# Per-head mean squares as rows of tokens, inverse roots spread by one fp32r product, and two maps folded in the transposition

## The reference

```python
x += 1/2 * post(SwiGLU_1(pre(x)))
x += post(W_out [GLA | DiffAttn+ALiBi | Retention](pre(x)))
x += 1/2 * post(SwiGLU_2(pre(x)))
...
o_a = _rms_norm(o_a, P['gla_norm'][l]) * silu(gr)           # 4 heads of 64
s = jnp.where(visible, s - slopes * dist, NEG_INF)
p = jax.nn.softmax(s, axis=-1)
a = p[:, 0] - lam * p[:, 1]                                 # two maps
return jnp.einsum('bhqk,bkhv->bqhv', a, vf)
...
o_d = _rms_norm(o_d, P['diff_subln'][l]) * (1.0 - lam_init) # 4 heads of 128
o_r = _layer_norm(o_r, P['ret_norm'][l]) * silu(rg)         # 4 heads of 64
```

## Time and profile before

| | |
|---|---|
| median of three runs | 1440.01 us |
| the profiled execution: its time, its span | 1441.2 us, 1439.4 us |
| mean granted TensorE clock | 0.977 |
| busy: TensorE, VectorE, ScalarE, GpSimd | 95%, 56%, 43%, 9% |
| chain that ended last, by engine | TensorE 86%, VectorE 6%, DMA 3%, ScalarE 2% |
| multiplications L582 to L584, all | 8016, 2512.3 us busy as records, which overlap |

### The profile page before, as it was taken

How to read it: one execution, slowest core, us unless ns; L and a number is a source line. 1 busy time by engine, 2 the same in 40 slices (tenths; PEclk the granted TensorE clock), 3 DMA queues, 4 the chain that set the end, 5 groups by cost and what they waited for, 6 DMA issues and landing times.

```text
span 1439.4 us, 24605 instructions
## 1 busy us (share of the span) xinstructions
PE 1369.2 (95%) x9589; PEld 1331.6 (93%) x9589; DVE 812.5 (56%) x1226; ACT 625.0 (43%) x987; POOL 122.7 (9%) x119
## 2 busy tenths in 40 slices
PE   5999999899999899999989999998899999999998
PEld 5999999887799899999989999988788999999998
DVE  5565544568654765554366555346765557655542
ACT  4444433552353654443354444346234455444343
POOL 0000000341000200000020000013500002000000
PEclk9999999999999999999999999999999999999999
DMA  5955445433241365545545555454232343555452
GB/s 145 272 147 153 143 146 150 123 99 88 80 125 46 97 182 151 153 140 148 153 115 147 147 146 149 149 172 104 61 89 78 110 118 102 146 149 154 140 147 75
DMA packets 351289, 188.50 MB, mean 131 GB/s; under 512 B 6188, under 2 KB 348472, under 8 KB 350968
## 3 DMA queue, kind: packets, MB, share of 16 engines
q1 hardware_dynamic: 348368, 177.49, 43.9%
q0 software_dynamic: 1872, 6.88, 1.4%
q10 hardware_dynamic: 984, 3.22, 0.7%
HBM read 183.25 MB, written 4.33 MB: 130 GB/s over the span
## 4 chain that ended last, share of the span: by engine, by line
PE 86%; DVE 6%; DMA 3%; ACT 2%; DVEq 1%; issue 1%; POOL 0%; ACTq 0%; SPq 0%; POOLq 0%
PE ps L582 26%; PE ps L584 26%; PE ps L583 25%; DMA raw<-in_ffn_w_up_dram 2%; DVE scores L1399 2%; DVE w_l L938 1%; DMA raw<-in_w_in_dram 1%; PE ps L860 1%; PE ps L870 1%; PE ps L638 1%; PE ps L763 1%; PE ps L834 0%; PE ps L748 0%; DVE y L1254 0%; PE ps L881 0%
## 5 line engine op out<-in xcount | busy, mean ns | idle before, releaser
L582 PE MATMUL ps<-xn_l,w_h 128*128 128x320 f32 x1840 | 588.2, 320 | 25.4 <-DVE xn_l L1243 18.2
L583 PE MATMUL ps<-xn_h,w_l 128*128 128x320 f32 x1840 | 576.4, 313 | 0.0
L584 PE MATMUL ps<-xn_h,w_h 128*128 128x320 f32 x1840 | 576.3, 313 | 0.0
L938 DVE TENSOR_TENSOR w_l<-raw,w_h 128x1024 fp32r<-128x1024 f32 (+1 forms) x342 | 412.5, 1208 | 185.0 <-ACT w_h L929 184.9
L929 ACT ACTIVATE w_h<-raw 128x1024 fp32r<-128x1024 f32 (+1 forms) x342 | 353.4, 1035 | 278.3 <-DMA raw<-in_ffn_w_down_dram 125.2
L582 PEld LDWEIGHTS ps<-xn_l,w_h 128*128 128x128 f32 x1840 | 353.2, 192 | 35.7 <-DVE xn_l L1243 19.6
L583 PEld LDWEIGHTS ps<-xn_h,w_l 128*128 128x128 f32 x1840 | 353.5, 192 | 0.8 <-issue 0.2
L584 PEld LDWEIGHTS ps<-xn_h,w_h 128*128 128x128 f32 x1840 | 353.1, 192 | 0.0
L582 PE MATMUL ps<-hid_l,w_h 128*128 128x320 f32 x704 | 217.4, 309 | 0.0
L584 PE MATMUL ps<-hid_h,w_h 128*128 128x320 f32 x704 | 217.3, 309 | 0.0
L583 PE MATMUL ps<-hid_h,w_l 128*128 128x320 f32 x704 | 217.3, 309 | 0.0
(11 more groups left out here) (223 smaller groups left out, 1165.8 us busy)
## 6 DMA issues: line engine op xcount, KB each, us to landing
raw<-in_ffn_w_up_dram SPq DMA_DIRECT2D x176, 512.0 KB, 3.9
raw<-in_ffn_w_down_dram SPq DMA_DIRECT2D x64, 448.0 KB, 3.7
raw<-in_w_in_dram SPq DMA_DIRECT2D x54, 512.0 KB, 3.8
raw<-in_ffn_w_down_dram SPq DMA_DIRECT2D x32, 512.0 KB, 3.9
raw<-in_w_out_dram SPq DMA_DIRECT2D x16, 512.0 KB, 4.1
const<-in_tables_dram ACTq DMA_DIRECT2D x1, 2176.0 KB, 10.7
mask_in<-in_masks_dram POOLq DMA_DIRECT2D x1, 1536.0 KB, 11.7
x_in<-in_x_prompt_dram SPq DMA_DIRECT2D x1, 1024.0 KB, 3.6
```

The source lines that it names most:

```text
L582: pe.matmul(out, w_h[s][:, w], xl, start=first, stop=False)
L583: pe.matmul(out, w_l[s][:, w], xh, start=False, stop=False)
L584: return pe.matmul(out, w_h[s][:, w], xh, start=False, stop=last)
L938: dve.tensor_tensor(w_l[s][:, 0:cols], raw[s][:, 0:cols], w_h[s][:, 0:cols], ALU.subtract).then_inc(w_lo, 1)
```

## The change

1. `stat` takes constants as the stationary operand: for each tile of squares a matrix `mean` of 128x44 that holds 1/64 or 1/128 in the columns of its heads, twice, at c and at 32 + c. One multiplication of 320 columns per tile is accumulated, so that the means stand as rows of 320 tokens, on 44 partitions (rows that no head has are zero). Root and reciprocal are then of 44x320, and VectorE adds two steps: a cast of the inverse roots to fp32r, and, for rows 32 to 43, the inverse root less its cast. The tile `inv_2` so holds each head's inverse root in two fp32r parts. Each step is followed by a drain. Storage for these rows is taken from tiles that are no longer used.
2. `spread` is one fp32r multiplication: `pick`, a 44x128 matrix of ones at the head's two rows, by `inv_2` of 44x320.
3. For the sample `att_t` is a multiplication of `probs` by `fold` (128x64, two identities on top of each other) in place of the transposition: it transposes and adds the two maps. `att_o` then needs three multiplications where it had six, and ScalarE copies 3x64 columns where it copied 3x128.
4. The tables grow: the second transfer has 4768 columns where it had 4352 (128 partitions, fp32), and `pick` is loaded by GpSimd's queue, 44x1024, behind the masks. TensorE waits for it once before the mixer.

```diff
@@ -49,11 +49,9 @@
-HEAD_AT = ((0, 2, "head64"), (2, 2, "head64"), (8, 1, "head128"), (9, 1, "head128"), (10, 1, "head128"), (11, 1, "head128"),
-           (4, 2, "head64"), (6, 2, "head64"))
+HEAD_AT = ((0, 2), (2, 2), (8, 1), (9, 1), (10, 1), (11, 1), (4, 2), (6, 2))
 HEAD_ORDER = (2, 3, 4, 0, 1, 6, 7, 5)
 STAT_HEADS = {"a": (0, 1, 6, 7, 2, 3, 4), "b": (5,)}
-STAT_COLS = {"a": (0, 11), "b": (11, 12)}
 STAT_BANK = {"a": 3, "b": 6}
@@ -222,6 +219,17 @@
     add("bias", np.concatenate([bias(r, r), bias(128 + r, np.arange(256)), b2], axis=1))
+    mean, pick = np.zeros((P, 8, 44)), np.zeros((P, 8, P))
+    for q, (c, w) in enumerate(HEAD_AT):
+        for h in range(w):
+            rows = slice(h * P // w, (h + 1) * P // w)
+            for g in (0, 32):
+                mean[rows, q, g + c + h] = w / P
+                pick[g + c + h, q, rows] = 1.0
+    fold = (r[:, None] % 64 == np.arange(64)[None, :]).astype(np.float32)
+    add("mean", mean.reshape(P, -1))
+    add("fold", fold)
+    add("pick", pick.reshape(P, -1))
     masks = []
@@ -253,7 +261,9 @@
         N_PAR = 16 * 10
+        NCONST -= 8 * P
         const = sb("const", [P, NCONST])
+        pick = sb("pick", [P, 8, P], F32R)
         mask = sb("mask", [P, 8, 3 * P], U8)
@@ -332,8 +343,10 @@
         tiny = place("tiny", [P, 32])
-        var_h = place("var_h", [P, 3, 12])
-        inv_h = place("inv_h", [P, 3, 12])
+        root_h = {"a": z[0:64, DQ[2], :], "b": decay[0:64, :]}
+        inv_h = {"a": z[0:64, DKK[2], :], "b": wgt_0[0:64, :]}
+        inv_2 = {"a": nc.alloc_sbuf_tensor_at("inv_2a", [P, T], F32R, offset=z0 + 4 * DV[2] * T),
+                 "b": nc.alloc_sbuf_tensor_at("inv_2b", [P, T], F32R, offset=qk_at)}
         assert here[0] <= nc.sbuf_usable_end, (here[0], nc.sbuf_usable_end)
@@ -508,6 +522,7 @@
                     pool.dma_start(mask_in[:, :], ins["masks"]).then_inc(masks_loaded, 16)
+                    pool.dma_start(pick[0:44, :, :].rearrange("p a b -> p (a b)"), ins["tables"][0:44, NCONST:]).then_inc(pick_loaded, 16)
                     pool.wait_ge(masks_loaded, 16)
@@ -844,7 +859,11 @@
                     for kt in range(KEYS[ATT[n][1]]):
-                        mm = pe.transpose(ps[:, 6, kt * P:(kt + 1) * P], probs[:, n % 2, kt * P:(kt + 1) * P], C("ident"))
+                        p = probs[:, n % 2, kt * P:(kt + 1) * P]
+                        if ATT[n][1] < 2:
+                            mm = pe.transpose(ps[:, 6, kt * P:(kt + 1) * P], p, C("ident"))
+                        else:
+                            mm = pe.matmul(ps[:, 6, kt * P:kt * P + T_S], p, C("fold"), start=True, stop=True)
                     mark("pe", mm, f"att_t{n}")
@@ -854,32 +873,22 @@
                         v = vc[:, kt, h * P:(h + 1) * P] if b == 2 and kt < 2 else dv_tok[:, kt, h, :]
-                        for m in range(1 if b < 2 else 2):
-                            o, a = (ps[:, 7, b * P:(b + 1) * P], probs_t[:, kt, :]) if b < 2 else \
-                                   (ps[:, 7, 256:320], probs_t[:, kt, half_rows(m)])
-                            mm = pe.matmul(o, v, a, start=b == 0, stop=b < 2 and kt == b or kt == 2 and m == 1, skip_group_check=True)
+                        o, w = (slice(b * P, (b + 1) * P), P) if b < 2 else (slice(T_P, T), T_S)
+                        mm = pe.matmul(ps[:, 7, o], v, probs_t[:, kt, 0:w], start=b == 0, stop=kt == b, skip_group_check=True)
                     mark("pe", mm, f"att_o{n}")
...
                     for q in STAT_HEADS[n]:
-                        c, w, ind = HEAD_AT[q]
-                        for i in range(3):
-                            at = 12 * i + c
-                            mm = pe.matmul(ps[:, STAT_BANK[n], at:at + w], z[:, q, TOK[i]:TOK[i] + P], C(ind), start=True, stop=True,
-                                           skip_group_check=True)
+                        mm = pe.matmul(ps[0:44, STAT_BANK[n], 0:T], C("mean")[:, 44 * q:44 * q + 44], z[:, q, :],
+                                       start=q == STAT_HEADS[n][0], stop=q == STAT_HEADS[n][-1])
                     mark("pe", mm, f"ms_{n}")
...
                     j = HEAD_ORDER.index(n)
-                    c, w, _ = HEAD_AT[n]
                     after(pe, l, "dve", "inv_b" if n == 5 else "inv_a")
                     after(pe, l, "dve", f"head{HEAD_ORDER[j - 2]}" if j >= 2 else "att_max11")
-                    m = P // w
-                    for i in range(3):
-                        for h in range(w):
-                            mm = pe.matmul(ps[h * m:h * m + m, 4 + j % 2, TOK[i]:TOK[i] + P],
-                                           inv_h[:, i, c + h:c + h + 1].broadcast_to([P, m]), C("ident"), start=True, stop=True)
+                    mm = pe.matmul(ps[:, 4 + j % 2, 0:T], pick[0:44, n, :], inv_2["b" if n == 5 else "a"][0:44, :], start=True, stop=True)
                     mark("pe", mm, f"spread{n}")
@@ -1019,7 +1029,7 @@
                 if l == 0 and f == 0:
-                    act.dma_start(const[:, FIRST:], ins["tables"][:, FIRST:]).then_inc(tables_loaded, 16)
+                    act.dma_start(const[:, FIRST:], ins["tables"][:, FIRST:NCONST]).then_inc(tables_loaded, 16)
                 with act.Fori(1, KF // 3 - 1) as i:
@@ -1113,7 +1123,8 @@
                         after(act, l, "pe", f"att_o{n - 1}")
-                    mark("act", act.activation(probs_t[:, 0:keys, :], ps[:, 6, 0:keys * P].rearrange("p (k c) -> p k c", c=P),
+                    w = P if ATT[n][1] < 2 else T_S
+                    mark("act", act.activation(probs_t[:, 0:keys, 0:w], ps[:, 6, 0:keys * P].rearrange("p (k c) -> p k c", c=P)[:, :, 0:w],
                                                ACT.Copy), f"att_t{n}")
@@ -1130,10 +1141,8 @@
                 elif kind == "stat":
-                    a, b = STAT_COLS[n]
-                    src = ps[:, STAT_BANK[n], 0:36].rearrange("p (i c) -> p i c", i=3)
                     after(act, l, "pe", f"ms_{n}")
-                    mark("act", act.activation(var_h[:, :, a:b], src[:, :, a:b], ACT.Sqrt, bias=C("eps")), f"sqrt_{n}")
+                    mark("act", act.activation(root_h[n][0:44, :], ps[0:44, STAT_BANK[n], 0:T], ACT.Sqrt, bias=C("eps")[0:44, :]), f"sqrt_{n}")
                 elif kind == "gates":
@@ -1488,9 +1497,12 @@
                 elif kind == "stat":
-                    a, b = STAT_COLS[n]
                     after(dve, l, "act", f"sqrt_{n}")
-                    mark("dve", dve.reciprocal(inv_h[:, :, a:b], var_h[:, :, a:b]), f"inv_{n}")
+                    dve.reciprocal(inv_h[n][0:44, :], root_h[n][0:44, :])
+                    dve.drain()
+                    dve.tensor_copy(inv_2[n][0:44, :], inv_h[n][0:44, :])
+                    dve.drain()
+                    mark("dve", dve.tensor_tensor(inv_2[n][32:44, :], inv_h[n][32:44, :], inv_2[n][32:44, :], ALU.subtract), f"inv_{n}")
                 elif kind == "spread":
```

More of the change, by code:

```diff
@@ L189, in constants @@
     add("lam", np.tile(np.concatenate([lam, 1.0 - lam])[None, :], (P, 1)))
+    add("pad", np.zeros((P, 2)))
     add("mean64", np.kron(np.eye(2), np.ones((64, 64))) / 64.0)
-    add("head64", np.kron(np.eye(2), np.ones((64, 1))) / 64.0)
-    add("head128", np.ones((P, 1)) / 128.0)
     rot = np.zeros((P, P))
@@ L323, in build @@
         wgt_0 = place("wgt_0", [P, T])
+        qk_at = here[0]
         qk_0 = place("qk_0", [P, 2, T])
@@ L359, in build @@
         tables_loaded = sem("tables_loaded")
+        pick_loaded = sem("pick_loaded")
         masks_loaded = sem("masks_loaded")
@@ L893, in _ @@
                 pe.wait_ge(tables_loaded, 16)
+                pe.wait_ge(pick_loaded, 16)
                 for kind, *arg in SCHEDULE:
```

## The result

The changed kernel takes 1448.7 us (median of 16 runs, 1444.2 to 1453.9), the kernel before beside it 1440.2 (16 runs, 1438.0 to 1447.6): 1.0059 times as long, with a 95% interval of 1.0049 to 1.0070. That is 8.5 us more. The forecast was 0.8 us less, so it was wrong by 9.3 us and on the wrong side. The ratios further down leave out two of the 21 runs of the kernel before that stand beside the last experiments, 1567.8 and 1685.3 us, whose mean granted clock was 0.81 and 0.75. The profiled execution took 1447.3 us, its span is 1445.5 (before 1439.4), the mean granted clock 0.972 (before 0.977). TensorE's share of the chain fell from 86% to 84%, VectorE's rose from 6% to 8%.

What follows compares the result with a forecast made beforehand. TensorE was taken as the bound, with VectorE setting the pace in places. Statistics and spreads -5.3, maps -2.5, clock +5.0, constants +2.0 gave -0.8 us: 1439.2 us predicted, range 1431 to 1446.

Steps and rivals of the forecast that it cites:

- VectorE's chain: Behind each statistics: root 0.43 to 0.48 us, reciprocal 2.1, cast 0.35, difference 0.48, gaps 0.2.
- Rival 3: VectorE's chain is longer and the kernel slower: 1446.8 us at 12 ns per column; chance 0.10 in the slower form.
- The statistics: Statistics `a` at the mixer's end: 14 records of 0.27 us, 3.8 us in all, without lowering the clock.
- TensorE's wait ahead of the spreads: After statistics `a`, TensorE waits 1.7 us for the inverse roots.
- Constants: Larger tables lengthen TensorE's wait in the first FFN by 1.0 us, clock fall costs 1.0: 2.0 us lost.
- Maps: Folded sample maps in the attention heads save 0.41 us per head, 2.5 us for three heads in two layers.
- rival 1: The clock stays up at these places and in the first FFN: 1433.2 us; chance 0.18.
- rival 2: TensorE's saving counts in full, with reciprocals ready in time: 1426 us; chance 0.14.
- both places that were named: Clock falls expected around 434.2 to 440.5, before `out` 0, and in the gap of about 4 us before `out` 2.
- rival 4: The change does not do what it says: fp32r spreads cost 0.15 us more each, under 1 us; chance 0.05.
- the term of the clock: Per layer, falls cost 1.5 us before `out` 0 and 1.0 around `out` 2, from one 3.4 us slow stretch.

Runs made afterwards that it cites:

- fill: Changed kernel plus eleven multiplications a layer that nobody reads, in TensorE's gaps ahead of the spreads and of `out` 2: 1441.7 us, 1.0014 of before.
- tables_only: Kernel before plus the larger tables and `pick`, with nothing reading them: 1442.7 us, 1.0017 of before.
- late_const: Changed kernel with `mean`, `fold` and `pick` loaded behind the first FFN's weights: 1448.4 us, 1.0048 of before.
- no_recip: Changed kernel with a copy of 44x320 in place of each reciprocal: 1438.0 us, 0.9986 of before.
- twice: Changed kernel with each reciprocal done twice, with a drain between: 1461.4 us, 1.0134 of before.

## Why the prediction was wrong

What held:

- VectorE's chain: reciprocal 2.14 (forecast 2.1), cast 0.32 (0.35), difference 0.48 (0.48), root 0.52 (0.43). Rival 3, a longer reciprocal, is refuted, though its sign was right. The Trainium skill's "VectorE: DVE Perf Modes", section "First, the fixed hardware budget", read as eight cycles for a column, gave 2.7 us as an estimate (it states a repeat count of 8, not a time); the trace disagrees: 2.14 / 320 is 6.7 ns with all fixed time in it.
- The statistics in 3.96 us and at the full clock; TensorE's wait ahead of the spreads, 1.56 (1.7), and ahead of `out` 2, 3.78 (about 4). From the second root to `out` 2 it took 4.23, forecast 4.25.
- Constants: 2.4 us for 2.0, though the wait in the first FFN was longer, 4.23 for 3.4. Maps: 3.8, where I had 2.5 outside the two stretches and 0.4 in each, 3.3.
- The clock falls at both places that were named, so rival 1 did not come, nor did rival 2: the inverse roots were late. A spread takes 0.25 us where I took 0.15, which rival 4 named; it is small.

What failed is the term of the clock, "2 x 2.5 = 5.0 us lost. Bounds: 0 (no fall) and 6.0". I priced each fall as one stretch like that at 287.9, 3.4 us long. The second fall was that long, the first twice as long, in both layers (443.0 to 449.8 and 1149.5 to 1156.3). The trace of the kernel before already had such lengths: between 25 and 1430 us its clock falls eleven times, and eight of these falls last over 6 us. One lies at its own statistics, and the earlier trace rows shows only its second half:

```profile
431.20:437.90 6.70, 6.70 (x30) 6.70 (x30) 0.36 (x1) 1.23 (x2) 0.00 (x0) 0.50 0.00 0
```

In the steps of layer 0, from the start of statistics `a`, in us (the forecast without the clock's term):

| to | before | forecast | measured | missing |
|---|---|---|---|---|
| the spreads | 9.85 | 7.5 | 7.70 | 0.2 |
| `out` 0 | 14.84 | 12.1 | 13.11 | 1.0 |
| second root | - | 17.0 | 20.05 | 3.1 |
| `out` 2 | 21.89 | 21.2 | 24.28 | 3.1 |
| `out` 3 | 25.88 | 23.8 | 28.09 | 4.3 |
| `out` 4 | 28.34 | 25.7 | 30.39 | 4.7 |

Most of what is missing is added where the clock is low. The first fall takes in the folded maps (1.24 for 0.64; 0.81 in layer 1, where the clock was still full), spread 4, `out` 0 (445.80 to 449.14, 3.34 for 1.76) and `att_o` (0.90 for 0.64); the second makes `out` 2 3.3 long. By the starts of these steps the clock costs about 3.7 us in this layer and 4.1 in the other (an estimate), 7.8 where I had 5.0. The rest is small steps that I had too short, among them 0.2 ahead of the spreads, and 0.4 from `out` 3 to `out` 4, which takes 2.30 here and 2.31 in `fill`, for 1.9. All together 4.7 are missing in this layer and 5.2 in the other (30.58 for 25.36), 9.9 where I had 5.0: 4.9 of the 9.3 us, 2.8 by the clock and 2.1 by small steps. `fill` shows the clock's part by itself: with TensorE busy in the gaps and nothing else in the program changed, 4.8 us come back in the same two stretches, though 3.4 us of low clock are left in each, and some 7 us in all.

Of the other 4.4 us the constants are 0.4. Their term too was too small where I can see it, in the wait (1.8 for 1.0) and in the clock behind it (low for about 6.8 us, for 1.0), but by `tables_only` an average run loses only 2.4 us to them. The maps gained 0.5 more than forecast, so 4.5 are left, which the runs don't locate; 2.4 of them is not in the two profiled executions at all, only in the medians. If the parts add, these us too hang on statistics and spreads: 9.9 us by the parts, and 10.5 come back with the reciprocal alone.

The price of the clock's term came from one fall in one place, and that was the mistake: falls last from 3.4 to 10 us in the runs here, at one place too (the second fall 3.4 us in the changed kernel's profile, 10 in that of `late_const`), and what stood behind the first was all of `out` 0 at nearly double the price. Also the gap and the fall are no separate costs: with a shorter chain there is less of both on average, which fits the 1.2 to 1.4 us for each us of chain in `no_recip` and `twice`. A single execution need not show it: in the profile of `no_recip` the clock of layer 0 is low for 10 us in all, as in the changed kernel. The Trainium skill's "TensorE: Matmul & The Clock Gate", section "Why this matters for your kernels", warns of idle gaps between bursts. `fill` agrees at the second place, its clock at 1.00 behind the filled gap and 0.54 without. The first fall came without one long gap: the waits ahead of it were 1.56 and 1.09 us, with short work between.

## What to carry to other kernels

Where TensorE is the bound, fewer multiplications are worth only what the other engines can follow: 42 short records for 14 saved 2.5 us each time, but the reciprocal of 320 columns in place of 33 costs VectorE 1.8 us, and in place of 3 columns 2.0, with a cast and a difference behind each (0.8), in front of everything that `w_out` waits for. Price a new gap in TensorE as the gap and half of the time that the clock then stays low while TensorE works (3 to 10 us in these runs), and put the range's end at the longer. Read the lengths of all falls in the trace, not of one. Test the parts of a change alone: here the maps were a gain, hidden below the loss of statistics, spreads and constants.

## What the runs showed of the hardware that I had not expected

- A reciprocal takes 2.14 us for 44x320 and for 12x320, where a copy takes 0.32: it goes by columns, not rows.
- TensorE's clock falls during unbroken work. Windows of the kernel before, the 42 short records of its statistics:

```profile
428.40:434.60 6.20, 6.20 (x44) 6.20 (x42) 0.87 (x2) 1.85 (x3) 0.00 (x0) 0.72 0.09 25
```

  TensorE is busy for all of it. The clock is 1.00 until 431.0, then 0.50 until 438, which gives 0.72 in this window and 0.50 behind it. With 14 records of 320 columns it is 1.00 all through. No run here separates the records' size from other reasons.
- More work can be less time: `fill` adds eleven multiplications a layer and is 7 us faster.
